# A hybrid S5, attention and PEER block on one core: the state scan as two real recurrences on phase-turned inputs, one score product per job, modulation rows summed by column groups and passed through memory

## The chip, the cores and the metric

The kernel runs on one core of one Trainium2 chip. A core has five engines with a queue each: TensorE (PE, matrix products into PSUM; its weight loads are shown as PEld), VectorE (DVE), ScalarE (ACT), GpSimd (POOL) and SyncE (SP, which here only issues transfers). The time is the device time of one execution in microseconds (us), the median over runs.

## The reference, cut to what matters

One layer on 512 tokens (T) of width 1024 (D), all float32:

```
mod = silu(c) @ w_ada + b_ada                        # 6 x 1024 numbers: sh1 sc1 g1 sh2 sc2 g2
h = x*(1+sc1) + sh1;  u, cq, ckv, kr = split(h @ w_in)       # 512, 384, 256, 32 columns
# S5: 32 groups of 16 channels with 64 complex states; a = exp((lam_re + i lam_im) dt)
s[t] = a*s[t-1] + Bb u[t];  y_s5 = glu(gelu(Re(C s) + d*u))
# attention: 8 heads; q and k are 64 plain and 32 rotated columns, k's rotated part is shared
q = rms(cq) @ w_uq;  k, v = rms(ckv) @ w_ukv
score = (q_nope.k_nope + rope(q_pe).rope(kr)) * scale, masked above the chunk (64 tokens) of the query
y_mla = softmax(score) @ v
x = layernorm(alpha*x + (1+g1) * (concat(rms(y_s5), rms(y_mla)) @ w_out));  h2 = x*(1+sc2) + sh2
# PEER: per token 8 heads choose 16 of 128*128 experts; gelu(u_tab[e].h2) * gate, summed over v_tab[e]
x = layernorm(alpha*x + (1+g2) * peer(h2))
```

## The kernel before

The program is six parts, each a block of its own with a barrier of all engines at its end: `condition`, `project`, `attend`, `mix`, `query` and `experts`. Within a block each engine runs the rows of its own queue in the order in which the code writes them, and waits on counted semaphores (`wait_ge`). Nothing is scheduled by a planner.

**condition** (0 to 119.5 us in the trace). `w_ada` comes in 12 pieces of 2 MB through three buffers, in the order `PART`. For pieces 0 to 3 PE multiplies (`modulation_row`, L428: the column `c_pad` is padded to 32 output rows and four such products stand side by side in the array), ACT evacuates, and PE sums the partial rows by a product with ones (`modulation_columns`). For pieces 4 to 11 DVE multiplies and adds, eight instructions of 128x512 a piece (L411, L412), into `mod_acc`; SP loads piece i from 7 on only when DVE has finished piece i-4. Between the rows PE runs `first_tiles` (L445: one row block of `w_in` against `hT` for six output tiles), then four more output tiles (L473). DVE also prepares the S5 constants: `powers(j)` multiplies C by the j-th power of a, and a loop of eight squarings gives the powers that the scan needs.

**project** (119.5 to 197.1 us). On PE, in this order: 32 transposes of `xr`, `xi` (L660), five products for the two rms norms (L669), 32 products that sum `mod_acc` into columns (L674), the rotated query part (L684: `w_qr` and its half-swapped copy `w_sw`), the plain query part (L689), small products for the S5 kernel matrix (L700), keys (L708), values (L715), and the chunk inputs of the scan (L725). DVE does reciprocals, norms, rotations and evacuations. `u` goes through memory (`u_scr`) to come back as `ut`.

**attend** (197.1 to 291.6 us). 32 jobs, (query block of 128 tokens) x (head), with 128, 256, 384 or 512 keys, eight jobs of each. A job on PE is three accumulated products, `kn` with `qn` (L747), `kpe` with `qr` (L748), and the mask as a product of two rows of one partition (L750); then, one job later, the transposes of the probabilities (L758), and two jobs later the product with `v` (L768). DVE takes the maximum (L846) and evacuates the transposed probabilities (`evac_probs`, L832); ACT does the exponential (L787). The scores have three PSUM banks. Beside the jobs runs the scan over 64 chunks as a doubling scan of complex numbers, six steps of which DVE does one half and POOL the other (L815 to L824, L865 to L871). Behind its last exponential ACT writes `spad` (L796), four instructions.

**mix** sums the S5 output, makes a row image of g1 by eight products (`gcol`, L1066), projects out and does the first layernorm. **query** computes the expert scores. **experts** has two halves: 128 blocks of `u_tab` against h2 (PE L1562 to L1564), in the second half of them with the weights by token (L1577, L1578), which ACT evacuates into `stage` (`evacuate_g`, L1503: 96 times, written with a step of 128 bytes between neighbours); then 128 blocks of `v_tab`. A `gcol2` product does for g2 what `gcol` does for g1.

Of the kernel before, what the change touches and what calls it, by code (L numbers as in the profile page):

```python
# [15 lines left out]
P = 128  # L16
# [33 lines left out]
NROWS = _n  # L50


class Plan:


    def __init__(self, nc):
        self.nc = nc
        self.u_scr = nc.dram_tensor("u_scr", (S5W, T), F32).ap()
        self.y_scr = nc.dram_tensor("y_scr", (S5W, T), F32).ap()
# [39 lines left out]
def place(k):  # L99
# [6 lines left out]
    k.consts = k.sb("consts", [P, 2], 1.8125)  # L106
# [27 lines left out]
    k.sv = k.sb("sv", [P, 24, NQ], 193)  # L134
    k.apr = k.sb("apr", [P, 9, NQ], 194.5)
    k.api = k.sb("api", [P, 9, NQ], 195.25)
    k.c_lay = k.sb("c_lay", [P, 2, NQ, GH], 196)
    k.dtmp = k.sb("dtmp", [P, 2, NQ, GH], 200)
    k.ptmp = k.sb("ptmp", [P, 2, NQ, GH], 202)
# [6 lines left out]
def one_plus(v, k, step, parts):  # L146

    for part in parts:
        at = k.modc[:, part * DK:(part + 1) * DK]
        step(v.tensor_scalar(at, at, 1.0, None, ALU.add))  # L150


def condition(nc, io, k, ps):

    k.s_cols, k.s_s5in, k.s_crep, k.s_ropein, k.s_ident, k.s_tab = k.sems("s_cols s_s5in s_crep s_ropein s_ident s_tab")
    k.modp_evac, k.mod_acc_ready, k.mod_tail, k.mod_cols, k.mod_read = k.sems("modp_evac mod_acc_ready mod_tail mod_cols mod_read")
    wa = [k.sem(f"w_ada_in{i}") for i in range(3)]
# [12 lines left out]
    def _(sp):  # L170
        def load_w_ada(i):
            if i >= 3:
                sp.wait_ge(k.mod_mm, i - 2) if i < 7 else sp.wait_ge(k.mod_acc_ready, i - 6)
            sp.dma_start(k.w_ada[:, i % 3], w_ada[:, :, PART[i] * 512:(PART[i] + 1) * 512]).then_inc(wa[i % 3], 16)
# [22 lines left out]
        sp.wait_ge(k.mod_acc_ready, 6)  # L197
        for kt in range(QK):
            sp.dma_start(k.w_qr[:, kt], w_uq[:, kt, :, NOPE:]).then_inc(k.s_wuq, 16)
            sp.dma_start(k.w_qn[:, kt], w_uq[:, kt, :, 0:NOPE]).then_inc(k.s_wuq, 16)  # L200
        sp.wait_ge(k.mod_acc_ready, 7)
        for kt in range(KK):
# [11 lines left out]
    LATER = [(k.kr32[:, :], slice(D_IN - ROPE, D_IN), 7), (k.ckvT[:, 0], slice(S5W + QL, S5W + QL + P), 0),  # L214
             (k.ckvT[:, 1], slice(S5W + QL + P, S5W + QL + KVL), 1), (k.cqT[:, 2], slice(S5W + 2 * P, S5W + QL), 2)]

    @k.block.scalar
    def _(act):
# [1698 lines left out]
```

## Time and profile before

| | us |
|---|---|
| median of 3 runs (1700.31 to 1704.53) | 1702.71 |
| the profiled execution: its own time | 1697.89 |
| its span in the trace | 1695.7 |
| busy PE, DVE, ACT, POOL | 1584.9, 1325.4, 715.2, 1007.4 |

The views below are of that one execution. The 2.2 us between its own time and its span lie outside the engines' work. Busy PE is made from modelled ends of overlapping products, so that a PE busy throughout need not be at its peak: what a product costs is read from one start to the next start.

### The profile page before, as it was taken

What the parts mean: (1) busy time and instruction counts of PE and PEld (TensorE: products, weight loads), DVE (VectorE), ACT (ScalarE), POOL (GpSimd) and SP (SyncE); (2) the same over time, 40 slices, a digit from 0 to 9 for tenths busy, and PEclk for the clock granted to TensorE, in tenths of its full rate; (3) what the DMA queues carried; (4) which work ended last, traced back from release to release, by engine and by line L of the source; (5) the groups of instructions that cost most, each with busy time, mean ns of one, the idle gap of its engine ahead of it and who ended that gap; (6) DMA issues with size and microseconds to landing.
All of it is one profiled execution on the core that took longest, in us unless ns stands there. A gap on an engine that the chain in (4) does not pass through costs nothing.

```text
span 1695.7 us, 22035 instructions
## 1 busy us (share of the span) xinstructions
PE 1584.9 (93%) x8095; PEld 1317.3 (78%) x8095; DVE 1325.4 (78%) x2052; ACT 715.2 (42%) x1241; POOL 1007.4 (59%) x623
## 2 busy tenths in 40 slices
PE   6969999896999999997999999989999999999994
PEld 2336776544889999997999999977788888888873
DVE  6975575157217999999988889639799999999997
ACT  1021223212224434434999999723233334333330
POOL 4402362001004677776766778868798999889863
PEclk9988879998999999998999999989999999999997
DMA  9592200723302677776899999999999999999971
GB/s 369 210 285 17 29 1 31 236 70 112 124 0 95 215 261 264 265 265 232 306 358 365 364 378 349 362 351 348 369 382 369 375 377 376 372 356 383 364 258 49
DMA packets 213642, 436.27 MB, mean 257 GB/s; under 512 B 34720, under 2 KB 127392, under 8 KB 211744
## 3 DMA queue, kind: packets, MB, share of 16 engines
q1 hardware_dynamic: 175952, 299.79, 50.2%
q0 software_dynamic: 36864, 134.23, 22.0%
q8 instruction: 64, 1.05, 0.2%
q10 hardware_dynamic: 720, 0.85, 0.2%
q14 instruction: 42, 0.34, 0.1%
HBM read 377.03 MB, written 56.62 MB: 256 GB/s over the span
## 4 chain that ended last, share of the span: by engine, by line
DVE 25%; DMA 15%; issue 11%; ACT 11%; POOL 4%; SPq 2%; PE 2%; POOLq 0%; DVEq 0%; ACTq 0%
DMA v_raw<-in_peer_v 7%; DMA u_raw<-in_peer_uT 5%; ACT hot1h L1495 4%; ACT stage L1503 3%; DVE wl L1774 3%; DMA a_in<-act_scr 3%; DVE ps L1658 2%; POOL vl L1456 2%; DVE junk L1650 2%; ACT uth L1467 2%; DVE w_f L1769 2%; DVE cand L1687 1%; DVE eq L1725 1%; DVE route L1726 1%; DVE idx L1685 1%
## 5 line engine op out<-in xcount | busy, mean ns | idle before, releaser
L1446 POOL TENSOR_TENSOR utl<-u_raw,uth 128x1024 fp32r<-128x1024 f32 x128 | 308.5, 2411 | 247.8 <-ACT uth L1467 247.2
L1562 PE MATMUL ps<-h2h,uth 128*128 128x384 f32 x1024 | 348.3, 340 | 0.9 <-POOL utl L1446 0.9
L1456 POOL TENSOR_TENSOR vl<-v_raw,vh 128x1024 fp32r<-128x1024 f32 x128 | 310.6, 2428 | 60.7 <-ACT vh L1467 58.5
L1564 PE MATMUL ps<-h2h,utl 128*128 128x384 f32 x1024 | 343.0, 335 | 0.0
L1563 PE MATMUL ps<-h2l,uth 128*128 128x384 f32 x1024 | 342.9, 335 | 0.0
L1586 PE MATMUL ps<-vh,wh 128*128 128x512 f32 x768 | 303.2, 395 | 14.7 <-DVE wl L1774 11.0
L1587 PE MATMUL ps<-vl,wh 128*128 128x512 f32 x768 | 302.2, 394 | 0.0
L1588 PE MATMUL ps<-vh,wl 128*128 128x512 f32 x768 | 301.8, 393 | 0.0
L1769 DVE TENSOR_TENSOR w_f<-a_in,g_in 128x384 f32<-128x384 f32 x128 | 218.8, 1710 | 52.1 <-DMA a_in<-act_scr 51.3
L1467 ACT ACTIVATE vh<-v_raw 128x1024 fp32r<-128x1024 f32 x128 | 135.3, 1057 | 195.6 <-DMA v_raw<-in_peer_v 179.4
L1562 PEld LDWEIGHTS ps<-h2h,uth 128*128 128x128 f32 x1024 | 192.9, 188 | 1.2 <-POOL utl L1446 1.2
L1563 PEld LDWEIGHTS ps<-h2l,uth 128*128 128x128 f32 x1024 | 193.0, 189 | 0.0
L1564 PEld LDWEIGHTS ps<-h2h,utl 128*128 128x128 f32 x1024 | 192.7, 188 | 0.0
L1586 PEld LDWEIGHTS ps<-vh,wh 128*128 128x128 f32 x768 | 146.3, 191 | 47.8 <-DVE wl L1774 9.9
L1588 PEld LDWEIGHTS ps<-vh,wl 128*128 128x128 f32 x768 | 146.2, 190 | 30.8
L1587 PEld LDWEIGHTS ps<-vl,wh 128*128 128x128 f32 x768 | 146.3, 191 | 30.3
L1658 DVE SCALAR_TENSOR_TENSOR ps<-ring,w_sp,ps 128x1024 f32<-128x1024 f32 x127 | 162.4, 1279 | 1.7
L1650 DVE CUSTOM_DVE_ANT_0 junk<-ring,ps 128x1024 bf16<-128x1024 f32 x128 | 150.0, 1214 | 17.3 <-DMA ring<-in_peer_u,row_at 17.2
L1441 POOL DMA_INDIRECT ring<-in_peer_v,row_at x128 | 137.5, 1074 | 23.2 <-issue 19.2
L1441 POOL DMA_INDIRECT ring<-in_peer_u,row_at x128 | 132.2, 1033 | 25.4 <-issue 13.5
L1467 ACT ACTIVATE uth<-u_raw 128x1024 fp32r<-128x1024 f32 x128 | 135.7, 1062 | 17.9 <-DMA u_raw<-in_peer_uT 17.5
L1479 ACT ACTIVATE acts<-ps 128x384 f32<-128x384 f32 x128 | 63.5, 496 | 165.0 <-PE ps L1564 164.9
(342 smaller groups left out, 2491.9 us busy)
## 6 DMA issues: line engine op xcount, KB each, us to landing
u_raw<-in_peer_uT SPq DMA_DIRECT2D x128, 512.0 KB
v_raw<-in_peer_v SPq DMA_DIRECT2D x128, 512.0 KB
w_ada<-in_w_ada SPq DMA_DIRECT2D x12, 2048.0 KB, 13.3
act_scr<-acts SPq DMA_DIRECT2D x64, 384.0 KB
g_scr<-stage SPq DMA_DIRECT2D x12, 2048.0 KB
g_in<-g_scr SPq DMA_DIRECT2D x32, 768.0 KB
a_in<-act_scr SPq DMA_DIRECT2D x64, 384.0 KB
w_q<-in_peer_w_query SPq DMA_DIRECT2D x8, 1024.0 KB, 6.8
```

The lines of the kernel that those rows point to most:

```text
L1441: nc.gpsimd.indirect_dma_start(k.ring[j % RING][:, :], None, table, bass.IndirectOffsetOnAxis(ap=k.row_at[:, slot:slot + 1], axis=0)).then ...
L1446: tt(k.utl[b % 3][:, :, :].rearrange(f3), k.u_raw[:, b % 4].rearrange(f3), k.uth[b % 3][:, :, :].bitcast(F32).rearrange(f3), ALU.subtract) ...
L1456: tt(k.vl[:, n % 4], k.v_raw[:, n % 4], k.vh[:, n % 4].bitcast(F32), ALU.subtract).then_inc(k.vl_done, 1)
L1467: copy = lambda dst, src: nc.scalar.activation(dst, src, ACT.Copy)
L1562: mm(o, hi, k.h2h[:, kt, SP:T], start=(kt == 0), stop=False)
L1563: mm(o, hi, k.h2l[:, kt, SP:T], start=False, stop=False)
L1564: ins = mm(o, lo, k.h2h[:, kt, SP:T], start=False, stop=(kt == DK - 1))
L1586: mm(o, hi, k.vh[:, n % 4, cols], start=(n == 0), stop=False)
L1587: mm(o, hi, k.vl[:, n % 4, cols], start=False, stop=False)
L1588: ins = mm(o, lo, k.vh[:, n % 4, cols], start=False, stop=(n == NBLK - 1))
L1658: ins = v.scalar_tensor_tensor(y_sp, row, w, y_sp, ALU.mult, ALU.add)
L1769: tt(k.w_f[:, n % 2].rearrange("p (c t) -> p c t", t=CHK), k.a_in[:, p % 2, n % 2].rearrange("p (c t) -> p c t", t=CHK), k.g_in[:, q % 2, ...
```

## The change

**Modulation.** Pieces 4 to 7 go to PE: rows 4, 5 and 6 stand behind `first_tiles(4)`, `(5)`, `(6)`, row 7 behind the first of the four later tiles, and ACT evacuates their partial rows into `mod_acc`. DVE keeps pieces 8 to 11. The sum in **project** is now eight products with 32 output rows and 512 columns, four column groups side by side, into banks 6 and 7; DVE adds the bias in two instructions (`modrow`); SP writes the rows to memory and reads them back as columns (`modc`) and, in **mix** and **experts**, as row images (`gate`, `gate2`). The products with `gcol` and `gcol2` are gone.

**Scan.** With B[c] turned by the angle of a^8 to the power -c, the complex recurrence over chunks becomes two real ones with the real factor |a|^8. DVE computes six doubled angles in **condition** (ACT their sines), a table `turn` of 64 angles in **project** by six doublings of six instructions, turns the inputs (six instructions of 128x1024), and runs two `tensor_tensor_scan` of 128x1040. In **attend** six instructions turn back. The six-step scan on DVE and POOL is gone, and the eight squarings too.

**Scores.** `qh` and `kh` hold for each head the 64 plain rows, the 32 rotated rows and 32 mask rows, so that one product of 128 rows gives the masked score. The mask rows come from memory. `evac_probs` moves from DVE to ACT, transposes follow two jobs behind the score and values three, and there are four score banks.

**Order.** In **project** the chunk inputs (L725 before) go ahead of the queries; their third bank waits for `modrow`. The S5 padding copies go from ACT to POOL, the squares from ACT to DVE. In **experts** the evacuation into `stage` reads PSUM with a step and writes runs of four numbers.

```
-            if i >= 3: sp.wait_ge(k.mod_mm, i - 2) if i < 7 else sp.wait_ge(k.mod_acc_ready, i - 6)
+            if i >= 3: sp.wait_ge(k.mod_mm, i - 2) if i < 11 else sp.wait_ge(k.mod_acc_ready, 1)
...
-        for i in range(4, 12):
+        for i in range(8, 12):
             dve.wait_ge(wa[i % 3], 16 * (i // 3 + 1))
             acc = k.mod_acc[:, (i - 4) * 512:(i - 3) * 512]
...
         for kt in range(4, DK):
             ins = first_tiles(kt)
+            if kt < DK - 1:
+                modulation_row(kt)
...
-        for m in range(16, NMOD):
-            ins = mm(ps[:, 7, m:m + 1], k.mod_acc[:, (m - 16) * P:(m - 15) * P], k.ones[:, 0:1], start=True, stop=True)
+        for r in range(2):
+            for g in range(4):
+                at = (4 * r + g) * 512
+                ins = mm(ps[32 * g:32 * g + 32, 6 + r, :], k.ones[:, 0:32], k.mod_acc[:, at:at + 512], start=True, stop=True,
+                         tile_position=(0, 32 * g))
         ins.then_inc(k.mod_tail, 1)
+        pe.wait_ge(k.a2_evac, 8)
+        pe.wait_ge(s_ut, 16 * CH)
+        for j in range(8):
+            part, b = j // 4, j % 4
+            if j >= 4:
+                pe.wait_ge(k.d2_evac, j - 3)
+            elif j == 2:
+                pe.wait_ge(k.modrow_ready, 1)
...
+        for r in range(2):
+            ins = v.scalar_tensor_tensor(k.modrow[:, r], ps[:, 6 + r], k.consts[:, 2 + r:3 + r], k.brow[:, r], ALU.add, ALU.add)
+        step.tell(ins, k.modrow_ready)
...
+        tt(t0, br, ts, ALU.mult)
+        tt(t1, bi, ts, ALU.mult)
+        tt(br, br, tc, ALU.mult)
+        step(tt(bi, bi, tc, ALU.mult))
+        tt(br, br, t1, ALU.add)
+        step(tt(bi, bi, t0, ALU.subtract))
+        for part, b in enumerate((k.ir, k.ii)):
+            w, m, b = (a.rearrange("p q c -> p (q c)") for a in (k.sct[:, part], k.mag[:, :, :], b[:, :, :]))
+            ins = v.tensor_tensor_scan(w, m, b, 0.0, ALU.mult, ALU.add)
...
-            mm(out, k.qn[:, h // 2, qb * P:n], k.kn[:, h, 0:n], start=True, stop=False)
-            mm(out, k.qr[:, h // 4, qb * P:n], k.kpe[:, h % 4, 0:n], start=False, stop=False)
-
-            mm(out[:, n - P // 2:n], k.negrow[0:1, :], k.onerow[0:1, :], start=False, stop=True).then_inc(k.sc_out, 1)
+            mm(ps[:, SB[i % 4], 0:n], k.qh[h // 4][:, h % 4, qb * P:n], k.kh[:, h, 0:n], start=True, stop=True).then_inc(k.sc_out, 1)
...
-            nc.scalar.activation(k.stage[:, ch % 2, :, at:at + HOTS].rearrange("p e t -> p t e"),
-                                 ps[:, 4 + n % 2].rearrange("p (t e) -> p t e", t=HOTS), ACT.Copy, scale=1.0 / W_UP).then_inc(k.g_evac, 1)
+            nc.scalar.activation(k.stage[:, ch % 2, :, at:at + HOTS],
+                                 ps[:, 4 + n % 2].rearrange("p (t e) -> p e t", t=HOTS), ACT.Copy, scale=1.0 / W_UP).then_inc(k.g_evac, 1)
```

What stands on PE from the norm products of **project** to its first query products (L669 and on) before:

```order
L669 MATMUL ps<-sq,ones 128x512 x5
L674 MATMUL ps<-ones,mod_acc 128x1 x32
L684 MATMUL ps<-cqn,w_qr 128x512 x3
L684 MATMUL ps<-cqn,w_sw 128x512 x3
L684 MATMUL ps<-cqn,w_qr 128x512 x3
L684 MATMUL ps<-cqn,w_sw 128x512 x3
L689 MATMUL ps<-cqn,w_qn 128x512 x12
```

And at the same place of the changed kernel:

```order
L756 MATMUL ps<-sq,ones 128x512 x5
L763 MATMUL ps<-mod_acc,ones 32x512 x8
L775 MATMUL ps<-ut,xtr 128x128 x16
L775 MATMUL ps<-ut,xti 128x128 x16
L785 MATMUL ps<-cqn,w_qr 128x512 x3
L785 MATMUL ps<-cqn,w_sw 128x512 x3
L785 MATMUL ps<-cqn,w_qr 128x512 x3
L785 MATMUL ps<-cqn,w_sw 128x512 x3
L790 MATMUL ps<-cqn,w_qn 128x512 x12
```

The 32 chunk-input products moved from the end of the part to here; the eight products of the third bank (half of the row with `xtr`) wait for `modrow_ready`.

DVE behind its last `mod_acc` piece, at the start of **project**, up to `modrow` in the changed kernel (six rounds of L667 to L672 stand there, the last one shown; the part began with the reciprocal before):

```order
L655 TENSOR_TENSOR sq<-cqT 128x512 x3
L655 TENSOR_TENSOR sq<-ckvT 128x512 x2
...
L667 TENSOR_TENSOR turn<-turn,turn_c 128x16x32
L668 TENSOR_TENSOR sct<-turn,turn_s 128x16x32
L669 TENSOR_TENSOR turn<-turn,turn_c 128x16x32
L670 TENSOR_TENSOR sct<-turn,turn_s 128x16x32
L671 TENSOR_TENSOR turn<-turn,sct 128x16x32
```

Everything in this fence now stands ahead of the reciprocals and of `modrow` on DVE.

The first jobs of **attend** on PE with 128 keys in the changed kernel; before, each job's single row L838 was the three rows L747, L748 and L750:

```order
L838 MATMUL ps<-kh,qh_96 128x128 x3
L846 MATMUL ps<-ident,prob 128x128
L838 MATMUL ps<-kh,qh_96 128x128
L846 MATMUL ps<-ident,prob 128x128
L856 MATMUL ps<-v,probT 128x64
```

Transposes now follow the score of the job two later, and values that of the job three later.

## Rows read from the trace of the kernel before

**Rows 1.** Windows of two stages: busy us (count) by engine, granted clock, DMA share, GB/s

```profile
119.50:197.10 77.60, 74.26 (x314) 49.93 (x315) 36.27 (x45) 20.78 (x37) 10.59 (x7) 0.86 0.37 43
...
796.00:1108.00 312.00, 308.18 (x2271) 298.27 (x2271) 258.13 (x240) 285.38 (x605) 235.20 (x143) 1.00 0.94 351
```

**Rows 2.** Timeline, end of condition: start, us, engine, line, work, idle before

```profile
118.44 0.75 DVE L412 SCALAR_TENSOR_TENSOR mod_acc<-w_ada,ccol,mod_acc 128x512 f32<-128x512 f32 x1
...
119.52 3.65 PE L660 MATMUL ps<-ident,xr 128*128 128x128 f32 x16 [11.58 <-PEq L1853]
```

**Rows 3.** Timeline, modulation and first tiles, PE and DVE in condition

```profile
36.15 1.92 PE L428 MATMUL ps<-w_ada,c_pad 128*32 128x512 f32 x16
...
55.49 22.56 PE L445 MATMUL ps<-hT,w_in 128*128 128x512 f32 x48 [1.98 <-DVE hT L333]
...
72.36 5.47 DVE L412 SCALAR_TENSOR_TENSOR mod_acc<-w_ada,ccol,mod_acc 128x512 f32<-128x512 f32 x7
```

**Rows 4.** Timeline of PE in project

```profile
132.12 11.45 PE L674 MATMUL ps<-ones,mod_acc 128*128 128x1 f32 x64
...
157.26 10.46 PE L689 MATMUL ps<-cqn,w_qn 128*128 128x512 f32 x24
...
188.60 3.73 PE L725 MATMUL ps<-ut,xtr 128*128 128x128 f32 x32
```

**Rows 5.** Timeline of DVE and POOL in project

```profile
131.32 3.35 DVE L610 RECIPROCAL rq<-rq 128x512 f32<-128x512 f32 x1 [12.13 <-ACT rq L587]
...
148.85 3.53 POOL L559 MEMSET m<- 128x4096 f32 x1
```

**Rows 6.** Timeline of DVE and POOL, instructions of 128x256 and one of 128x1024

```profile
58.25 0.80 POOL L300 TENSOR_TENSOR ptmp<-xi,apr 128x256 f32<-128x256 f32 x1
58.49 0.83 DVE L384 TENSOR_TENSOR dtmp<-zn,api 128x256 f32<-128x256 f32 x1
...
62.25 0.42 DVE L384 TENSOR_TENSOR dtmp<-zn,api 128x256 f32<-128x256 f32 x1
...
382.52 1.23 DVE L1037 TENSOR_TENSOR x<-x,ln_g 128x1024 f32<-128x1024 f32 x1
```

**Rows 7.** Timeline of PE in attend, one job of 512 keys and the next start

```profile
279.84 1.08 PE L747 MATMUL ps<-kn,qn 128*128 128x512 f32 x2
280.75 1.02 PE L748 MATMUL ps<-kpe,qr 128*128 128x512 f32 x2
281.70 0.43 PE L750 MATMUL ps<-onerow,negrow 1*128 1x64 f32 x2
282.06 0.66 PE L758 MATMUL ps<-ident,prob 128*128 128x128 f32 x4
282.56 1.00 PE L768 MATMUL ps<-v,probT 128*128 128x64 f32 x8
283.39 1.08 PE L747 MATMUL ps<-kn,qn 128*128 128x512 f32 x2
```

**Rows 8.** Groups by form in attend: count, busy us, mean ns, idle before

```profile
L846 DVE TENSOR_REDUCE nmax<-ps 128x1 f32<-128x256 f32 x8 | 3.4, 421 | 5.6 <-PE ps L750 5.6
...
L787 ACT ACTIVATE prob<-ps,nmax 128x256 f32<-128x256 f32 x8 | 3.8, 474 | 20.3 <-DVE nmax L846 20.3
...
L796 ACT ACTIVATE spad<-ir 64x1024 f32<-64x1024 f32 x2 | 2.1, 1049 | 0.0
```

**Rows 9.** Windows, attend whole and its slow part, columns as in rows 1

```profile
197.10:291.60 94.50, 91.57 (x432) 65.18 (x432) 64.71 (x96) 25.12 (x69) 51.16 (x25) 0.84 0.00 1
...
199.30:230.30 31.00, 30.03 (x104) 23.21 (x103) 23.44 (x32) 5.41 (x22) 26.57 (x12) 0.50 0.00 1
```

**Rows 10.** Timeline, 32 transposes of mix on PE

```profile
403.87 5.51 PE L1102 MATMUL ps<-ident,x 128*128 128x128 f32 x32 [10.19 <-POOL x L960]
```

**Rows 11.** Groups by form, the evacuation into stage in 796 to 1108

```profile
L1503 ACT ACTIVATE stage<-ps 128x512 f32<-128x512 f32 x96 | 102.1, 1165 | 0.0
```

**Rows 12.** Groups by form, an ACT evacuation with a step in condition

```profile
L256 ACT ACTIVATE uT<-ps 128x512 f32<-128x512 f32 x4 | 2.1, 602 | 31.4 <-PE ps L445 31.4
```

More of the change, by code:

```diff
@@ L50 @@
 NROWS = _n
+TURNS = 6
 class Plan:
@@ L353, in _ @@
         modulate(0)
+        for i in range(TURNS):
+            ins = v.tensor_scalar(k.turn_x[:, i], sv["th"], float(CH << i), None, ALU.mult)
+        step(ins)
+        reduce_angle(k.turn_x[:, :, :], k.turn_s[:, :, :], k.turn_c[:, :, :], k.turn_k[:, :, :], k.turn_red)
         dve.wait_ge(k.sin_ready, 1)
@@ L570, in _ @@
                 half = slice(g2 * NS, (g2 + 1) * NS)
-                ins = nc.scalar.activation(k.bpad[half, part, :, g2, :], x[half, :, CH - 1, :], ACT.Copy)
+                ins = nc.gpsimd.tensor_copy(k.bpad[half, part, :, g2, :], x[half, :, CH - 1, :])
         ins.then_inc(k.bpad_ready, 1)
+        pool.wait_ge(k.bpad_ready, 1)
+        pool.wait_ge(k.s_wuq, 16 * (HEADS + QK))
+        w_qr, w_sw = (w[:, :, :, :, :, :].rearrange("p k i two h c -> p (k i two h) c") for w in (k.w_qr, k.w_sw))
+        nc.gpsimd.tensor_copy(w_sw[:, :, 0:H2], w_qr[:, :, H2:])
+        nc.gpsimd.tensor_copy(w_sw[:, :, H2:], w_qr[:, :, 0:H2]).then_inc(k.wsw_ready, 1)
+        nc.gpsimd.memset(k.m1[:, :, :], 0.0).then_inc(k.m1_zero, 1)
+        pool.wait_ge(k.d2_out, 8)
+        nc.gpsimd.memset(k.spad[:, :, :, :, :], 0.0).then_inc(k.spad_zero, 1)
+    @k.block.scalar
+    def _(act):
         n = 0
@@ L608, in _ @@
         kcol = k.cols[:, ROW_AT["mla_kv_norm"]:]
+        for i in range(QK + KK):
+            x = k.cqT[:, i] if i < QK else k.ckvT[:, i - QK]
+            tt(k.sq[:, i], x, x, ALU.mult).then_inc(k.sq_ready, 1)
+        dve.wait_ge(k.a2_out, 8)
+        dve.wait_ge(k.bpad_ready, 1)
+        tc, ts = k.turn[:, 0], k.turn[:, 1]
+        v.memset(tc[:, :, 0:1], 1.0)
+        step(v.memset(ts[:, :, 0:1], 0.0))
+        for i in range(TURNS):
+            n = 1 << i
+            c, s = (a[:, i].unsqueeze(2).broadcast_to([P, NQ, n]) for a in (k.turn_c, k.turn_s))
+            c0, s0, c1, s1 = tc[:, :, 0:n], ts[:, :, 0:n], tc[:, :, n:2 * n], ts[:, :, n:2 * n]
+            t0, t1 = k.sct[:, 0, :, 0:n], k.sct[:, 1, :, 0:n]
+            tt(c1, c0, c, ALU.mult)
+            tt(t0, s0, s, ALU.mult)
+            tt(s1, s0, c, ALU.mult)
+            step(tt(t1, c0, s, ALU.mult))
+            tt(c1, c1, t0, ALU.subtract)
+            step(tt(s1, s1, t1, ALU.add))
+        v.tensor_copy(k.mag[:, :, 1:], k.mag8[:, :].unsqueeze(2).broadcast_to([P, NQ, NC]))
+        step(v.memset(k.mag[:, :, 0:1], 0.0))
         dve.wait_ge(k.a2_evac, 9)
@@ L889, in place_mix @@
     k.gate = k.sb("gate", [P, D], 115)
-    k.gcol = k.sb("gcol", [P, DK, P], 119)
     k.yT = k.sb("yT", [P, SK, CH, NC], 131)
@@ L1531, in _ @@
                 weigh_high(m, half)
-            if b == G_LAST + 2:
-                act.wait_ge(k.gate2_out, 1)
-                for half in range(2):
-                    ins = copy(k.gate2[:, half * 512:(half + 1) * 512], ps[:, 4 + half])
-                ins.then_inc(k.gate2_evac, 1)
             if b >= NBLK - 2:
@@ L1607, in _ @@
                 weights_by_token(n)
[L1608 to L1615 removed]
+        pe.wait_ge(k.g_evac, GROUPS4)
         for n in range(LAST4):
@@ L1880, in by_state, with mask_rows @@
     return np.ascontiguousarray(np.stack(halves, axis=1))
+def mask_rows():
+    rows = np.zeros((2, ROPE, T), np.float32)
+    for r in range(TT):
+        rows[0, r, r * P:r * P + P // 2] = 1.0
+        rows[1, r, r * P + P // 2:(r + 1) * P] = MASKED
+    return rows
 def by_block(u):
```

410 lines of the change are left out of this document (205 added, 205 removed).

## The prediction

> **What bounds the kernel now.** I read the windows of the stages first, then in each stage the timeline of its last waits, then the groups by form for durations. The engine that sets the end differs by stage.
>
> In **condition** DVE ends last. PE has been idle for 11.58 us when the barrier opens at 119.52; the last `mod_acc` instruction ends at 118.44 + 0.75 = 119.19 [rows 2]. In **project** PE is busy 74.3 of 77.6 us, DVE 36.3 [rows 1]: PE sets it. In **attend** PE is busy 91.6 of 94.5 us [rows 9]. A job with 512 keys is a chain without a gap on PE: starts at 279.84, 280.75, 281.70, 282.06, 282.56, next job at 283.39, so 0.91 + 0.95 + 0.36 + 0.50 + 0.83 = 3.55 us [rows 7]. DVE's scan steps and POOL's run beside it. In the second half of `u_tab` (796 to 1108) PE is busy 308.2 of 312.0 us, ACT 285.4, the DMA share is 0.94 [rows 1]: three resources near full, PE first. There the reader is to see that a gain on ACT alone is worth little.
>
> **The change, part by part.** The profiled execution took 1697.89; the median of the runs is 1702.71, 4.8 above it. I sum differences and subtract them from the median. 0.3% is 5.1 us, about what a measurement of this kernel can tell from no change.
>
> *Condition.* A piece on DVE is one 0.48 us instruction and seven in 5.47 us [rows 3]: 5.9 us. Four leave, 23.7 us less, so DVE no longer ends last as long as its last pieces arrive. PE gains four modulation rows of 1.92 us [rows 3], 7.7 us. It also starts `first_tiles(4)` some 2 us earlier: PE idled 1.98 us before 55.49 for `hT` [rows 3], which stands behind two fewer `powers` steps on DVE. PE ended at 119.52 - 11.58 = 107.9, so it now ends near 107.9 - 2.1 + 7.7 = 113.5. DVE's last two pieces come in by about 102 and cost 11.8: it ends near 109 to 114, hidden at best by a few us. I take 113.4 instead of 119.5: **-6.1**, from -8 (clock not falling in the earlier gap) to -4 (last piece late).
>
> *Project.* The 32 column products, two passes each, took 11.45 us [rows 4]; eight products with 32 output rows and 512 columns take by the modulation row's pace (16 in 1.92) about 1.9 with their second passes: -9.5. The chunk inputs move, unchanged in cost. But now their third bank waits for `modrow`, and behind that wait on PE's queue stand the queries, kernel matrix, keys and values, everything that is left. `modrow` comes late because DVE does the turn table ahead of it. DVE's time there: an instruction costs 0.15 + 1.05 ns per element, from 0.42 us at 256 and 1.23 us at 1024 [rows 6]. Five squares of 512 take 3.4, ending about +5.5 us from the start of the stage. Six doublings of six instructions with 16 to 512 elements come to 11.8 so costed, 8.9 if the 0.08 overlap of neighbours holds; I take 10.3. A copy of the factors is at most 1.2: +17.0. Two reciprocals, about 2.1 for the three instructions of `cqn` (512 elements each, as costed above) and 1.4 for the two of `ckvn`, the reciprocals at 3.35 [rows 5]: +27.2; two `modrow` instructions of 0.65: **+28.5**. PE, without the 9.5, would have come to this wait near +18 to +20 (it waits for `ut` from memory first). It stalls 8 to 10 us. From there: six more banks at 3.73 / 4 = 0.93 [rows 4], 5.6, with some 2.7 lost to a lower clock behind the idle time, +36.8. Queries to values took 188.60 - 143.57 = 45.0 before [rows 4], of which the rotated part took 157.26 - 143.57 = 13.7, though it has as many products as the plain part in 10.46: 3.2 lost to the lower clock, which I let go now. 41.9 more, +78.7, and the barrier: 79.3 instead of 77.6: **+1.7**. Both ends: -2 (the cheap price of the doublings and the stall 3 shorter) and +8. The high end is contention: DVE took 0.83 for a 128x256 instruction while POOL did the same kind of work, and 0.42 without it [rows 6]. POOL's memset takes 3.53 [rows 5], and in the changed kernel a memset and copies of POOL lie beside the turn table; doubled doublings alone would be +10, of which I count at most 6. Behind `modrow` DVE has rotations, turned inputs, two scans and the evacuations of keys; their unknown price (a 128x1040 scan lies between an instruction of 1024 elements, 1.23, and its double or more) is hidden while PE works 42 us; that cover is some 2 us tight at the end for `kh`.
>
> The Trainium skill, "SBUF — State Buffer", section "Who interferes with whom", says that a DVE instruction with two SBUF inputs contends with a GpSimd instruction that reads SBUF and not with one that only writes it. By that rule the memset costs the turn table nothing and only the padding copies count, so that the high end would be nearer +4 than +8. The doubled instruction above has a reading neighbour and agrees; no row shows one beside a memset.
>
> *Attend.* One product of 0.91 replaces 0.91 + 0.95 + 0.36: a job with 512 keys falls from 3.55 to 0.91 + 0.50 + 0.83 = 2.24 us on PE; 384: 1.68; 256: 1.12; 128: 0.56 at full clock. There is a floor by latency, since a job's values wait for maximum, exponential and copy: at 256 keys score 0.42, `nmax` 0.42, exponential 0.47 [rows 8], a copy of the same size at about 0.42 and some 0.25 between; three jobs in flight over it leave a period of some 1.3, at 128 keys 1.1; jobs of 384 and 512 are PE-bound. The clock counts too: it was 0.50 (1.2 GHz) from 199.3 to 230.3 with PE busy 30.0 of 31.0 us [rows 9], and full for the rest, as 0.84 over the whole stage says. I let it rise after the first eleven jobs as before, which now is some 19 us in. Sum: lead-in 1.3; eight of 128 at 1.15 and 2.0 for the turn-back instructions of 1.23 [rows 6] in DVE's queue, 11.2; eight of 256 at 1.3 and three of them 0.88 more for the half clock, 13.0; eight of 384, 13.5; eight of 512, 18.0; from the last score to the barrier 5.8, as ACT's four `spad` copies of 1.05 [rows 8] now stand behind the last `evac_probs`. 62.8, I take 63.1: **-31.4**. Ends: -36 (full clock soon, no floor) and -19 (half clock through the jobs with 384 keys).
>
> The Trainium skill, "TensorE: Matmul & The Clock Gate", section "Part 4: PE-mode transpose", says that a transpose doesn't count as busy for the clock gate, and that full clock does not engage for it. The row says otherwise: 32 transposes alone, behind 10.19 us of idle time, took 5.51 us [rows 10], where 32 at the half-clock pace (twice 0.50 / 4, 0.25) would take 8.0; so the clock rose within them. By the page's rule attend, with a larger share of transposes now, would stay longer at the half clock, and its gain would be that of the second case below.
>
> *Mix and query.* The products with `gcol` leave PE where it waits for the S5 output anyway: **0** (1 either way).
>
> *Experts.* In 796 to 1108 PE is idle 3.8 us in all [rows 1]; a cheaper evacuation can give back no more there. `stage` costs 1165 ns [rows 11]; an evacuation of the same size from PSUM read with a step, written in runs, takes 602 [rows 12], so ACT is relieved by up to 54 us that nothing waits for. `gcol2` leaves 1 to 2 us of PE, and 0.5 MB of `gate2` image joins a DMA that moves 351 GB/s, +1.4 at most. Together **-2.5** (0 to -6).
>
> Sum: -6.1 + 1.7 - 31.4 + 0 - 2.5 = -38.3. 1702.7 - 38.3 = 1664.4, rounded 1665 (profiled near 1660).
>
> **The rivals.**
> 1. *The clock rises later in attend.* If it takes 31 us of work rather than eleven jobs, all jobs of 256 and one or two of 384 stay at half: +6 to +12. For it: PE was busy throughout those 31 us and still at half [rows 9], and the short jobs now leave more gaps. Against: at other restarts it rose within a few us [rows 10]. Total 1671 to 1677.
> 2. *Half clock throughout attend.* Eight each at 1.15, 2.24, 3.36, 4.48 make 90, with lead-in and tail 99: attend gains nothing and the whole is -2, 1701. Against: 61 us of the same mix ran at full clock before.
> 3. *`modrow` later still.* If DVE's turn table takes double beside POOL or `kh` comes behind PE, +10: 1675.
> 4. *The experts gain more than PE's idle time shows*, since PE and DMA both move on when ACT is freed, over 900 us of pairing: -14, 1650. Against: DMA at 0.94.
> 5. *Slower.* The stepped PSUM read in `stage` could be the dearer form. ACT has 312.0 - 285.4 = 26.6 us of room over 96 instructions, 0.28 each. From 1.44 us each the stretch becomes ACT-bound; it cancels the 38 us at 1165 + 280 + 400 = 1.84 us; at double, 2.33, it costs 85 and gives about 1750. Against: the stepped `uT` evacuation at 602 ns is as cheap as a plain one.
> 6. *It does not do what it says*: the score product of 128 rows costs as much as the two it replaces (1.86); then attend gains only the mask, 32 x 0.3, and the total is near 1690. Against: 0.91 and 0.95 for 64 and 32 rows alike [rows 7]: columns set the cost.
>
> **Chances.** Forecast 0.58 (1655 to 1671), rival 1 0.20, rival 2 0.04, rival 3 0.07, rival 4 0.06, rival 5 0.02, rival 6 0.03. The range of eight in ten takes the forecast, rivals 1 and 3: 1651 to 1681. Faster takes all but rivals 2 and 5, and a share of what is near: 0.95; same 0.03; slower 0.02.
>
> **What would show it.** Project should start near 113.4 with DVE or PE a few us ahead of each other; in it PE should be idle 8 to 10 us before the third bank of chunk inputs, released by `modrow` near +28.5, and the stage should last 79. Attend should last 63, with jobs of 512 keys 2.24 apart and granted clock 0.50 only in the first 20 us; a rise at 30 us is rival 1. `stage` should be near 600 ns with PE's idle time in that stretch below 2 us. The prediction is wrong if attend's floor by latency lies above the PE time of the wide jobs, if a wait in project exceeds 15 us, or if experts moves by over 6 us.

## The result, and the profile after

| | before | changed |
|---|---|---|
| median of the runs (us) | 1701.51 (4 runs, 1695.94 to 1704.53) | 1650.05 (4 runs, 1647.91 to 1650.62) |
| profiled execution: own time, span | 1697.89, 1695.7 | 1649.95, 1648.2 |
| condition, project, attend (us) | 119.5, 77.6, 94.5 | 115.0, 77.3, 56.1 |
| from mix to the first product with `uth`, from there to the end (us) | 232.6, 1171.4 | 233.1, 1166.7 |

The ratio is 0.9699 (95% interval 0.9672 to 0.9726): 51 us faster, where 38 were forecast, and 1 us below the range of the forecast (1651 to 1681). The profiled executions differ by 48. Stages are counted from the first PE instruction behind one barrier to that behind the next.

The windows of the changed kernel: condition, project, attend, and the second half of `u_tab`. Columns: stretch and length; busy us (instructions) of PE, PEld, DVE, ACT, POOL; granted clock; DMA share; GB/s.

```profile
0.00:114.96 114.96, 98.41 (x325) 39.45 (x325) 77.21 (x157) 18.41 (x35) 35.54 (x68) 1.00 0.89 306
114.96:192.25 77.29, 62.59 (x266) 38.21 (x267) 61.23 (x102) 18.58 (x32) 11.74 (x9) 0.89 0.45 64
192.25:248.10 55.85, 49.02 (x304) 38.26 (x304) 25.23 (x46) 35.31 (x101) 0.00 (x0) 0.97 0.00 1
...
753.00:1065.00 312.00, 310.82 (x2286) 301.71 (x2285) 259.57 (x240) 247.10 (x606) 237.88 (x143) 1.00 0.95 358
```

Attend's granted clock is 0.97 where it was 0.84 [rows 9]; the forecast had it at half for the first 20 us of the stage. Project is as long as in the trace before, though PE is busy 11.7 us less than in [rows 1]. In the last row, to be read beside 796 to 1108 us of [rows 1], PE is idle 1.2 us instead of 3.8, ACT is busy 38 us less, and the DMA rate is 358 instead of 351 GB/s.

PE's timeline in project, with each wait:

```profile
114.96 1.94 PE L747 MATMUL ps<-ident,xr 128*128 128x128 f32 x16 [0.93 <-PEq L1903]
...
122.87 1.92 PE L763 MATMUL ps<-mod_acc,ones 128*32 128x512 f32 x16
134.16 3.75 PE L775 MATMUL ps<-ut,xtr 128*128 128x128 f32 x16 [9.37 <-DMA ut<-u_scr]
142.31 3.79 PE L775 MATMUL ps<-ut,xtr 128*128 128x128 f32 x16 [4.39 <-DVE modrow L690]
145.88 3.79 PE L775 MATMUL ps<-ut,xti 128*128 128x128 f32 x32
```

The reader sees two waits in a row: for `ut`, until 19.2 us into the stage, and for `modrow`, until 27.35 (forecast: 28.5). The group of products behind each wait runs at half pace: 3.75 and 3.79 us for 16 instructions, against 3.79 for 32 right after.

PE's timeline in attend shows three things. The eight jobs with 128 keys take 6.5 us (192.25 to 198.80). Behind them, among the jobs with 256 keys, lies the only stretch at the half clock, where a product takes 1.17 instead of 0.65 us. Two jobs with 512 keys are 2.19 us apart (forecast 2.24):

```profile
192.25 0.91 PE L838 MATMUL ps<-kh,qh 128*128 128x128 f32 x6 [0.94 <-PEq L1903]
...
198.80 0.65 PE L838 MATMUL ps<-kh,qh 128*128 128x256 f32 x2
...
205.34 1.17 PE L838 MATMUL ps<-kh,qh 128*128 128x256 f32 x2
...
207.46 0.65 PE L838 MATMUL ps<-kh,qh 128*128 128x256 f32 x2
...
236.41 1.08 PE L838 MATMUL ps<-kh,qh 128*128 128x512 f32 x2
237.33 0.60 PE L846 MATMUL ps<-ident,prob 128*128 128x128 f32 x4
...
238.60 1.08 PE L838 MATMUL ps<-kh,qh 128*128 128x512 f32 x2
```

### The profile page after: what moved, and what is told of

The parts are those of the page before. It is cut to its first block, busy times and chain, and to the rows that moved or that the text cites. A ratio compares the mean times of both kernels' runs of the same rounds, so it can differ in the third digit from the quotient of the medians.

```text
span 1648.2 us, 21717 instructions
## 1 busy us (share of the span) xinstructions
PE 1532.8 (93%) x7951; PEld 1275.6 (77%) x7951; DVE 1287.7 (78%) x2005; ACT 686.8 (42%) x1270; POOL 957.5 (58%) x599
## 3 DMA queue, kind: packets, MB, share of 16 engines
q0 software_dynamic: 36864, 134.23, 22.5%
## 4 chain that ended last, share of the span: by engine, by line
PE 43%; DVE 18%; DMA 4%; issue 3%; POOL 1%; SPq 1%; ACT 0%; POOLq 0%; DVEq 0%; ACTq 0%
PE ps L1642 9%; PE ps L1643 9%; PE ps L1644 9%; PE ps L1618 5%; PE ps L1620 5%; PE ps L1619 4%; DVE junk L1700 2%; DMA a_in<-act_scr 2%; DMA v_raw<-in_peer_v 1%; PE ps L1633 1%; DVE cand L1737 1%; PE ps L1634 1%; DVE eq L1775 1%; DVE route L1776 1%; DVE idx L1735 1%
## 5 line engine op out<-in xcount | busy, mean ns | idle before, releaser
L1642 PE MATMUL ps<-vh,wh 128*128 128x512 f32 x768 | 302.4, 394 | 17.9 <-DVE wl L1824 14.3
L1819 DVE TENSOR_TENSOR w_f<-a_in,g_in 128x384 f32<-128x384 f32 x128 | 231.7, 1811 | 55.5 <-DMA a_in<-act_scr 54.2
L1642 PEld LDWEIGHTS ps<-vh,wh 128*128 128x128 f32 x768 | 145.6, 190 | 51.5 <-DVE wl L1824 12.3
L1700 DVE CUSTOM_DVE_ANT_0 junk<-ring,ps 128x1024 bf16<-128x1024 f32 x128 | 150.0, 1214 | 13.5 <-DMA ring<-in_peer_u,row_at 13.3
```

Of the source, the lines that this page charges most:

```text
L1642: mm(o, hi, k.vh[:, n % 4, cols], start=(n == 0), stop=False)
L1700: ins = v.tensor_tensor_reduce(out=k.junk[j % 2][:, :], in0=row, in1=y_sp, scale=1.0, scalar=0.0, op0=ALU.mult, op1=ALU.add, accum_out=k.d ...
L1819: tt(k.w_f[:, n % 2].rearrange("p (c t) -> p c t", t=CHK), k.a_in[:, p % 2, n % 2].rearrange("p (c t) -> p c t", t=CHK), k.g_in[:, q % 2, ...
```

## The experiments

Two questions stood open after the result: why the half clock in attend had gone, and why the experts and the medians had moved more than the sum said. Ratios are to the kernel before, measured beside each run on the same chip; its median lay from 1701.5 to 1706.0 us from chip to chip, so ratios compare better than medians. The length of attend is from its first PE instruction to the first of mix.

**The kernel before once more (e1).** No edit.

> The kernel before, unchanged, for a second trace. Theory A (the slow stretch of TensorE's clock in attend belongs to this program): granted clock 0.50 for about 31 us in attend again, attend 94 to 95 us, and the runs spread over some 8 us because of the length of such stretches. Theory B (it was an accident of one execution): attend at full clock, 79 to 82 us. If the stretch varies by 5 us or more between the two traces, that is the difference between the profiled execution (1697.9) and the median (1701.5).

Ratio 0.9998 (0.9979 to 1.0016). Windows of its attend, whole and in part:

```profile
195.10:296.50 101.40, 96.10 (x432) 67.94 (x432) 63.97 (x96) 25.12 (x69) 50.47 (x25) 0.80 0.00 1
...
229.00:245.00 16.00, 16.00 (x55) 11.71 (x54) 8.19 (x14) 2.44 (x9) 5.28 (x4) 0.55 0.00 1
```

Half clock again, and for longer, some 41 us: attend took 101.7 us, 7 more than in the trace that the prediction read, and e11, whose attend is that of the kernel before, took 102.0. The stretch belongs to this program and its length varies. The trace that the prediction read had a short stretch, which is part of why it lay below the median.

**The old work of a score on the changed kernel (e2, e3, e6, e9).** Four kernels that differ only in the score products of a job:

```
             q, kk = k.qh[h // 4][:, h % 4, qb * P:n], k.kh[:, h, 0:n]
+            mm(out, q, kk, start=True, stop=False)               # e2, e3, e6; e9 has one
             mm(out, q, kk, ...)
+            mm(out[:, n - P // 2:n], k.ones[0:1, 0:P], k.ones[0:1, 0:P // 2], ...)     # e2, e9: one row
+            mm(out[:, n - P // 2:n], q[:, 0:P], kk[:, 0:P // 2], ...)                  # e6: 128 rows
```

Each changes the scores, so the attention's values are others; the amount of all later work is the same.

> The changed kernel with the work of a job's scores as before: the score product twice, accumulated, and a product of one row with 64 columns (the scores come out doubled). Lags, banks and engines stay changed. Theory A (the clock falls for long because of what the old score products are): half clock again for 20 to 35 us, attend 80 to 92 us. Theory B (full clock comes from the deeper pipeline and the four banks): full clock but for a few us, attend 56 + 18 for the second product + 10 for the small ones, less what the latency floor hid = 76 to 84 us; jobs of 512 keys 3.4 to 3.5 apart.

> The changed kernel with the score product of each job twice, accumulated (scores doubled), without the one-row product. If columns set the cost, each adds 0.23, 0.46, 0.68 or 0.91 us by width, 18.2 us over the 32 jobs, of which the short jobs hide 2 to 4: +14 to +18, about 1665. Theory A (the clock, by small one-row products): full clock here and half in the run with three. If the clock falls here too, +25 to +35.

> As the run with three products, but the third of 128 rows and 64 columns instead of one row and 64 columns (the scores are other sums). Same number of instructions and columns. Theory A1 (one row of weights is what matters): full clock, attend 80 to 84 us, total 1672 to 1676 with a narrow spread. Theory A2 (a third small product on a PE without gaps is enough): half clock as with the one-row product, total 1680 to 1700, wide spread.

> The changed kernel with its single score product, and a one-row product of 64 columns behind it in each job (it adds 1 to half of the scores). Theory A (one-row products bring the half clock): granted clock 0.50 for 20 to 40 us of attend, +11 for the products and +10 to +20 for the clock, 1670 to 1680, wide spread. Theory B (the half clock needs two full products beside it): full clock, +6 to +11, 1656 to 1661, narrow spread.

| run | products of a job | median, range of runs | ratio (interval) | attend |
|---|---|---|---|---|
| changed | 1 | 1650.1, 1647.9 to 1650.6 | 0.9699 (0.9672 to 0.9726) | 56.1 |
| e3 | 2 | 1664.4, 1662.5 to 1665.6 | 0.9784 (0.9766 to 0.9803) | 68.5 |
| e6 | 2 and a small one of 128 rows | 1666.8, 1662.8 to 1668.1 | 0.9784 (0.9759 to 0.9810) | 73.3 |
| e2 | 2 and a small one of one row | 1685.1, 1671.4 to 1698.5 | 0.9881 (0.9821 to 0.9940) | 101.7 |
| e9 | 1 and a small one of one row | 1686.0, 1679.5 to 1692.7 | 0.9892 (0.9862 to 0.9923) | 86.5 |

Windows inside attend, of e2, then of e6, then of e9:

```profile
220.00:230.00 10.00, 10.00 (x34) 7.33 (x34) 2.07 (x5) 2.25 (x9) 0.00 (x0) 0.50 0.00 0
```

```profile
220.00:230.00 10.00, 10.00 (x61) 7.75 (x60) 3.03 (x6) 4.53 (x14) 0.00 (x0) 1.00 0.01 2
```

```profile
222.00:232.00 10.00, 10.00 (x32) 6.41 (x31) 1.54 (x3) 2.73 (x9) 0.00 (x0) 0.50 0.01 2
```

e2 and e6 have the same queues and the same number of instructions and columns; what differs is the small product, which has 1 row in e2 and 128 in e6 (and so other operands too). With one row PE stays at 0.50 while it is busy 10.0 of 10.0 us; with 128 rows it is at 1.00. The price of the one-row product in e9 is 30 us of attend, where e6 against e3 gives 4.8 us for a small product of the same columns: some 25 us are the clock. e2's profiled execution is the longest of its four, e9's the shortest of its four, and both show the half clock.

The one-row product does not bring the long stretch in every execution. Over the whole execution the mean granted clock was 0.959 and 0.957 in the two long runs of e2 (1698.5 and 1695.9 us), and 0.972 and 0.973 in the two short ones (1674.3 and 1671.4), which is the level of e6 (0.970 to 0.974). In e9 all four were low, 0.945 to 0.959, and in the kernel before all were at 0.965 or less. So runs spread by 27 us in e2, 13 in e9 and 8 to 12 in the kernel before, against 3 in e3 and 5 in e6. What decides it within one kernel stays open.

A second full product (e3) costs 12.4 us of attend and 14.3 of the median, not 18.2: short jobs hide part of it. That a product of 128 rows costs no more than one of 64 is read from the changed kernel itself, 0.92 us at 512 keys (236.41 to 237.33) against 0.91 [rows 7].

**The kernel before without a one-row product (e5, e13).** e5 drops the mask product (scores unmasked); e13 keeps a product in its place, of 128 rows (scores with another sum in them):

```
-            mm(out[:, n - P // 2:n], k.negrow[0:1, :], k.onerow[0:1, :], start=False, stop=True)
+            mm(out[:, n - P // 2:n], k.qn[:, h // 2, qb * P:n], k.kn[:, h, 0:P // 2], start=False, stop=True)    # e13
```

> The kernel before without the one-row mask product of each job (the scores are not masked). By PE time alone: 32 x 0.36 us at full clock, 32 x 0.4 in part at half, so -11.5 to -14, with the half clock staying for 30 us or more and the runs spreading by 8 us. Theory A (the one-row products go with the half clock): full clock in attend but for a few us, attend near 94.5 - 12 - 15 = 66 to 72 us, total -25 to -32, and a narrow spread. Theory B (what counts is how closely PE is packed, or the engines beside it): the half clock stays, total -12 to -15.

> The kernel before with its one-row mask product replaced by a product of 128 rows and the same 64 columns (the scores are not masked but get another sum). No product less, no column less. Theory A (the one-row product brings the half clock, in this kernel too): granted clock 1.00 in nearly all of attend; the scan on DVE and POOL then sets the first 45 us as in the run without a mask product, attend 85 to 90 instead of 94 to 97, total -6 to -10. Theory B (the half clock comes of the rest of this kernel, and the run without mask products escaped it by having fewer of them): attend 94 to 97, total 0.

e5: 0.9949 (0.9930 to 0.9968), attend 84.8. e13: 0.9943 (0.9923 to 0.9963), attend 86.9. Windows of e13, its whole attend and its first part:

```profile
197.40:284.10 86.70, 73.55 (x432) 58.22 (x432) 69.68 (x96) 25.09 (x69) 56.37 (x25) 0.94 0.00 1
```

```profile
206.00:216.00 10.00, 7.20 (x30) 6.33 (x30) 8.37 (x12) 1.88 (x8) 9.70 (x5) 0.53 0.00 0
...
226.00:236.00 10.00, 8.01 (x49) 6.57 (x48) 10.00 (x10) 1.70 (x6) 9.27 (x4) 1.00 0.01 2
```

The half clock lasts some 10 us instead of 31 or more, in the kernel before too, with no product less; e5, with a product less, shows 10 us as well, so dropping the product did no more to the clock than giving it 128 rows. What brings these 10 us no run shows. The last row shows a second thing: PE is busy only 8 of 10 us, DVE 10.0 and POOL 9.3. I read this as the old scan, which lay behind the slow PE and sets the pace as soon as PE is fast. The runs agree that both had to go: attend took 101.7 us with the old scan gone and the one-row product in place (e2), 86.9 with the scan in place and no one-row product (e13), and 73.3 with neither and just as many products (e6). e6 also has the deeper pipeline and the copies of probabilities on ACT, so the last step is not the scan's alone. My expectation for e5 (total -25 to -32) overlooked this second limit.

**The lags (e7).** Transposes one job behind and values two, as before:

```
-            if 2 <= i < len(jobs) + 2:
-                transposes(i - 2)
-            if i >= 3:
-                values(i - 3)
+            if 1 <= i <= len(jobs):
+                transposes(i - 1)
+            if i >= 2:
+                values(i - 2)
```

> The changed kernel with transposes one job behind the score and values two, as before; ACT evacuates one job behind. If the deeper pipeline carries the gain: the latency of score, maximum, exponential, transpose, copy shows in each job; short and middle jobs at 1.9 to 2.1 us instead of 0.9 to 1.6, attend +15 to +20. If the product count carries it: 0 to +6. The gaps on PE may also bring the half clock back; then +20 to +30.

0.9682 (0.9653 to 0.9711), median 1649.7, attend 56.4: no difference that can be told. The deeper pipeline carries nothing of the gain that these runs can tell.

**The evacuation into stage (e4, e11).** e11 puts the new form into the kernel before, as shown; e4 does the reverse in the changed kernel:

```
-            nc.scalar.activation(k.stage[:, ch % 2, :, at:at + HOTS].rearrange("p e t -> p t e"),
-                                 ps[:, 4 + n % 2].rearrange("p (t e) -> p t e", t=HOTS), ACT.Copy, ...)
+            nc.scalar.activation(k.stage[:, ch % 2, :, at:at + HOTS],
+                                 ps[:, 4 + n % 2].rearrange("p (t e) -> p e t", t=HOTS), ACT.Copy, ...)
```

> The changed kernel with the evacuation into stage written with the step, as before. stage 1165 ns instead of 582, ACT +56 us in that half, PE's waits for it 3.7 instead of 1.2. Theory A (the experts' 4.8 us come mostly from this): +2.5 to +4. Theory B (they come from gcol2 leaving PE and ACT's time is free): 0 to +1.

> The kernel before with the evacuation into stage read with the step and written in runs, nothing else. Undoing this in the changed kernel cost 7.4 us. If it is worth the same by itself: -6 to -8. If it was worth that only because gate2 and other edits load the same stretch: 0 to -3.

e4: 0.9746 (0.9730 to 0.9763), median 1657.5, 7.4 above the changed kernel. e11: 0.9944 (0.9924 to 0.9963), 9.3 us below the kernel before. Its group by form in the kernel e11, to be read beside 1165 ns [rows 11]:

```profile
L1503 ACT ACTIVATE stage<-ps 128x512 f32<-128x512 f32 x96 | 51.9, 585 | 0.0
```

From the first to the last start of a product of `h2h` with `uth`, the five traces with the old form (before, e1, e4, e5, e13) took 600.1 to 607.4 us, mean 603.7, and the twelve with the new one 592.8 to 599.1, mean 596.0 (changed 593.9, e11 594.6). The two groups don't overlap, and ACT's time was worth some 8 us there though it was not the fullest engine. The first 275.5 us of that stretch, before the first evacuation into `stage`, are alike in all traces (PE idle 9.6 us). In the rest PE is idle 4.7 us (before) to 8.7 with the old form and 0.5 to 5.3 with the new one, by the means 6.5 and 2.6. So half of the 8 us is idle time of PE, and the other half lies in PE's busy time, whose cause no run separates. PE's waits that name `stage` add up to only 3.7 us in the kernel before and 1.2 in the changed one. e4's list of waits from 753 to 1100 us has beside them one of 2.4 us for `utl`, which is 0.2 in the changed kernel:

```profile
PE ps L1633 <- ACT stage L1564: 4.1, 5, 2.0
...
PE ps L1618 <- POOL utl L1511: 2.4, 1, 2.4
```

POOL's `utl` waits for ACT's `uth` 81.8 us in that stretch of e4 and 68.1 in the changed kernel. That ACT's lateness reaches PE by POOL as well is how I read it; no run separates it.

**The pieces of the modulation (e10, e14, e15).** Pieces 4 to 7 back on DVE in the changed kernel; e14 is the changed kernel itself beside it.

```
-        for i in range(8, 12):
+        for i in range(4, 12):
             dve.wait_ge(wa[i % 3], 16 * (i // 3 + 1))
...
-            if kt < DK - 1:
-                modulation_row(kt)
```

> The changed kernel with pieces 4 to 7 of the modulation back on DVE, all else kept. If the change of place is what shortens condition: DVE ends condition again near 119 to 121, PE idle about 9 us ahead of the barrier, total +4 to +6. Rival (condition's length follows from the loads of w_ada and varies by itself): within 2 us.

> The changed kernel, unchanged, in the same call and on the same chip as its variant: ratio to the kernel before 0.968 to 0.972 again. It is the base against which the next run is read.

> The changed kernel with pieces 4 to 7 on DVE again, for a comparison on one chip. By the stages seen so far (condition 117.4 instead of 111.6 to 117.5 in seven traces, mean 115.0; project 78.1 instead of 77.3): +2 to +4 above the run beside it. By my prediction's sum (4 pieces and the earlier start together 6.1): +5 to +7.

e10: 0.9706 (0.9681 to 0.9730), median 1654.8. e14: 0.9684 (0.9655 to 0.9713), median 1646.1. e15: 0.9750 (0.9726 to 0.9774), median 1658.3, 12.2 above e14. By the ratios the move back costs 1 to 4 us in e10 and 11 in e15, so the whole time sizes it badly; the stages do it better. Condition took 117.4 and 117.9 us with the pieces on DVE, and in ten traces with them on PE 111.6 to 117.5, mean 114.7; two traces of the kernel before and three of its variants gave 119.5 to 123.0, mean 121.3. So the move is worth 3 us in this stage, and all edits of the stage together 6.6.

Condition and project have to be read together, since in the kernel before a long condition goes with a short project: 121.2 to 123.0 with 73.5 to 74.0 us in three traces, 119.5 and 119.8 with 77.6 in two. Attend began at 195.1 to 197.4 us there (mean 196.5), at 190.0 to 195.3 in the eight traces with the changed condition and project (mean 192.0), and at 195.5 and 197.0 with the pieces on DVE. The move is worth some 4 us by this count, about all that the two stages gain.

Of the 12.8 us between the spans of e14 and e15, 4.5 lie in condition, 2.6 in project and attend, and 5.4 in the first half of experts (592.8 against 598.2), which the edit does not touch. e14's is the shortest of the twelve traces with the new form, and e10 took 598.4. Whether the pieces have a part in that stays unexplained.

**Two attempts to fill project (e8, e12).** e8 moves `modrow` ahead of DVE's reciprocals, the second reciprocal and `ckvn` behind the copies of the chunk inputs, and the bias loads behind those of `ut`:

```
+        dve.wait_ge(k.s_brow, 64)
+        for r in range(2): ins = v.scalar_tensor_tensor(k.modrow[:, r], ps[:, 6 + r], ...)
         step(v.reciprocal(k.rq[:, :], k.rq[:, :]))
...
-        dve.wait_ge(k.s_brow, 64)
```

> The changed kernel with DVE's modrow ahead of both reciprocals, the second reciprocal and ckvn behind the chunk copies, and SP's four loads of the bias behind those of ut. If my account of project is right, ut lands 2 us sooner (+17), modrow is ready at +17 to +18, PE's 4.4 us wait for it is gone and the 9.4 us wait for ut is 7.4: project 71 us, total -5 to -7. Rival: DVE becomes late for the rotated queries or keys and takes it back, -2 to +2.

0.9677 (0.9652 to 0.9702), median 1646.8; project 78.0. No gain that can be told, where 5 to 7 us were expected. Timeline of PE and DVE in it:

```profile
131.71 5.69 PE L776 MATMUL ps<-ut,xtr 128*128 128x128 f32 x32 [10.29 <-DMA ut<-u_scr]
141.49 5.46 PE L776 MATMUL ps<-ut,xti 128*128 128x128 f32 x32 [4.09 <-DVE ir L708]
...
133.72 1.41 DVE L679 SCALAR_TENSOR_TENSOR modrow<-ps,consts,brow 128x512 f32<-128x512 f32 x2 [6.38 <-DMA brow<-in_b_ada]
```

The rival came: the bias now landed 22 us into the stage, DVE idled 6.4 us for it, and its chunk copies came so late that PE waited 4.1 us for them instead of 4.4 for `modrow`. `ut` did not land sooner (+20.1).

e12 puts work into the gap instead: the kernel-matrix products stand ahead of the chunk inputs, the bias is loaded between the store of `uT` and the loads of `ut`, `modrow` keeps the place that it has in e8, and ACT's `spad` copies lie between exponentials:

```
+        pe.wait_ge(k.bpad_ready, 1)
+        for b in range(4):                      # into banks 4, 5, 2, 3; ACT evacuates
+            ... mm(out, k.bpad[...], z[:, q, 0:CH]...)
+        pe.wait_ge(k.kt_evac, 4)
         pe.wait_ge(s_ut, 16 * CH)
...
+            if i in (16, 19, 22, 25):           # ACT, between exponentials
+                nc.scalar.activation(k.spad[half, part, :, g2, :], (k.ir, k.ii)[part][half, :, 0:NC], ACT.Copy)
```

> The changed kernel with: the kernel-matrix products ahead of the chunk inputs, into banks 4, 5, 2, 3, evacuated by ACT; bias loads between the store of uT and the loads of ut; modrow on DVE ahead of both reciprocals, rkv and ckvn behind the chunk copies; ACT's four spad copies between exponentials of jobs 16 to 25. PE's wait for ut (9.4 us) holds 7.1 us of products, the 4.4 us wait for modrow is gone, attend's tail is 3.5 us shorter: project 66 to 68 us, attend 52.5, total -12 to -15, about 1636. Rivals: contention of DVE's and ACT's later work moves the wait to keys or to the m loads (-5); ACT's copies delay exponentials (attend +2).

0.9563 (0.9545 to 0.9580), median 1630.9, below the changed kernel by 1.2 to 1.4% of the time before, some 21 to 23 us. Project and attend both came out shorter than in e8 and in the changed kernel. Windows of its project and attend:

```profile
114.93:177.66 62.73, 58.52 (x266) 34.94 (x267) 58.98 (x98) 20.95 (x36) 11.73 (x9) 1.00 0.61 79
177.66:230.90 53.24, 48.18 (x304) 36.96 (x304) 25.23 (x46) 34.97 (x101) 0.00 (x0) 1.00 0.00 1
```

Project fell by 14.6 us, 3.1 more than the 7.1 and 4.4 counted. The clock is 1.00 instead of 0.89: PE's gap before the chunk inputs is 3.3 us and they run at full pace (3.81 us for 32), where two groups of 16 took 3.75 and 3.79. The two groups at full pace are some 3.7 us less, an estimate from these lines, which covers the rest.

## Why the prediction was wrong

The sum was 13 us short: -38.3 forecast, -51.5 by the medians (-47.5 by the two spans). The mechanism that carried most of it, one product for three in each job, was right; terms of the sum were mis-sized. Between the two spans the misses are 7.0 us in attend, 2.2 in experts and 2.0 in project, less 1.5 in condition and 0.5 in mix and query; another 4 are the base.

- **Attend, -31.4: measured -38.4. This is the step that failed, and in it the price of the short jobs.** "Lead-in 1.3; eight of 128 at 1.15 and 2.0 for the turn-back instructions" makes 12.5 us; measured 6.55. The jobs with 256 keys took 12.4 for 13.0, with 384 12.9 for 13.5, with 512 and the tail 24.3 for 23.8. Two things lie in the short jobs:
  - *The floor by latency, with lead-in and turn-back.* e10, whose attend is that of the changed kernel, had full clock throughout: its sixteen jobs with 128 and 256 keys took 17.6 us. At full clock the forecast's own terms (1.3, eight at 1.1, 2.0, eight at 1.3) make 22.5, so 4.9 of the miss are here. The parts that the forecast names for a job with 256 keys add up to 1.98 us, and three jobs in flight over that give 0.66, not the 1.3 that it took.
  - *The clock.* "I let it rise after the first eleven jobs as before" cost 3.0 us in the sum (eight jobs at 1.15 and not 1.1, and 0.88 more in three). The clock was at half for some 3.5 us, not 19, and the sixteen jobs took 18.9 instead of 17.6: 1.3 us, so 1.7 of the miss are here. Half for longer would not have given the forecast's time: in e15, with the same attend, half clock for 10 us gave 19.3, where the forecast had 25.5.

Lines of PE in e10, then in e15; the jobs with 384 keys begin 17.58 and 19.34 us behind the first product:

```profile
195.52 0.91 PE L833 MATMUL ps<-kh,qh 128*128 128x128 f32 x6 [0.94 <-PEq L1898]
...
213.10 0.86 PE L833 MATMUL ps<-kh,qh 128*128 128x384 f32 x2
```

```profile
197.00 0.91 PE L833 MATMUL ps<-kh,qh 128*128 128x128 f32 x6 [0.94 <-PEq L1898]
...
204.78 1.17 PE L833 MATMUL ps<-kh,qh 128*128 128x256 f32 x2
...
216.34 0.86 PE L833 MATMUL ps<-kh,qh 128*128 128x384 f32 x2
```

- **The half clock as a habit of the stage.** I took it for given and gave a chance of their own only to longer stretches; both rivals on the clock went the wrong way. The low end of attend, -36 ("full clock soon, no floor"), is what came, and 2.4 us more. That the stretch goes with one of the products removed I never priced.
- **The base.** I subtracted from the median, rightly, but sized the gain on an execution whose half-clock stretch was short. Attend took 94.5, 101.7 and 102.0 us in the three traces that have the attend of the kernel before, so a typical gain there is nearer 43. This can account for the 4 us between medians and spans, though the stages vary against each other.
- **Experts, -2.5 (0 to -6): measured -4.7, and 8 in the first half by the means over traces.** The step "a cheaper evacuation can give back no more there" than PE's idle 3.8 us is refuted by e11, where that evacuation alone is worth 9.3 us (interval 0.37 to 0.76%, 6 to 13 us). The window of 312 us ended before the half did, with 0.9 us of idle time behind it; the trace was the shortest of five in this half; and about half of the gain is not idle time of PE at all. `stage` at 582 ns was as forecast (600). Rival 4 named this effect, at a chance of 0.06. Its total of 1650 is met by luck: most of what the forecast lacked came from attend.
- **Condition, -6.1, and project, +1.7: measured -4.6 and -0.3 here; by the means over traces -6.2 and +1.7.** Both terms held; between the two profiled traces they look off only because the base had a short condition and a long project. The start of `first_tiles(4)` did not come earlier (55.40): PE idled 1.29 us for `hT` there, and DVE had itself waited 0.80 us for PE's column products before it.
- **Inside project.** Nearly every time held: the turn table and the copy of the factors until +15.8 (forecast 17.0), `modrow` at +27.35 (28.5). `ut` came at +19.2 and the two banks behind it ran at half pace, so PE reached the wait for `modrow` at +23.0, not +18 to +20, and idled 4.4 us in it, not 8 to 10. The end of that wait is DVE's, so the length of the stage did not change by it.
- **Rivals 2, 5 and 6** are excluded: by the clock of 0.97, by 582 ns, and by 0.92 us for the score product of 128 rows.

The turn table met POOL's memset of the changed kernel at 119.93 to 123.43. DVE's instructions of 128x128 in it took 0.28 to 0.29 us with and without that neighbour. The Trainium skill, "SBUF — State Buffer", "Who interferes with whom", said so: a GpSimd instruction that only writes does not contend. The trace agrees, and my high end of +8 for project had no ground in the memset. The other page that I weighed, "TensorE: Matmul & The Clock Gate", "Part 4: PE-mode transpose", would have had attend's 80 transposes hold the clock down; 0.97 here, and 1.00 throughout attend in e8, e10 and e12 with the same transposes, speak against it.

## What to carry to other kernels

When a stretch of a profile runs at the half clock, ask which kind of product in it is special before taking it as given, and try that product in another shape; here a product with a single row of weights, repeated in every job, cost far more by the clock than by its own time. Take the base of a sum from more than one execution, stage by stage: here it moved attend by 7 us, condition by 3, project by 4 and the experts' first half by 7. Work a floor by latency out from its parts and check the quotient, since it is easily taken twice too high. When a wait for memory opens a gap on PE, put independent products into it: here that gave back the gap and the slow restart behind it.

## What the hardware showed that I had not expected

- A 64-column product of one row in each job held the granted clock at 0.50 (1.2 GHz) for 31 to 48 us of an almost gapless PE (31 us in the trace before, some 41 in e1, 44 in e2, 48 in e9, where PE was busy 10.0 of 10.0 us in most windows). With 128 rows in its place there was no such stretch in e6, and about 10 us of it in the kernel before (e13). By the mean clock two of e2's four executions escaped it.
- In short jobs the half clock costs little: 10 us of it in e15 made sixteen jobs 1.8 us longer than in e10.
- The same 512-element evacuation on ACT takes 1165 ns when it writes with a step of 128 bytes and 582 to 586 ns when it reads PSUM with a step and writes runs of four.
- Two `tensor_tensor_scan` of 128x1040 take 2.32 and 2.30 us on DVE, nearly twice the 1.23 us of a plain instruction of 1024 elements [rows 6].
